# Last attention unit and first output strip of a two-layer decoder step: other order on four engines

## The reference

```
proj = u @ w_in;  q, gate = proj[..., :2048], proj[..., 2048:]
log_keep = where(mask, log_sigmoid(-z), 0);  suffix = sum of log_keep over later keys
attn = where(mask, exp(log_sigmoid(z) + suffix), 0);  o = attn @ v
out = (o * silu(gate)) @ w_out;   x = x + rms_norm(out, g_post)
```

## Time and profile before

| | |
|---|---|
| median of 3 runs | 1904.2 us (1903.65 to 1906.14) |
| the profiled execution's own time | 1900.16 us |
| its span | 1898.4 us |
| mean granted TensorE clock | 0.957 |
| TensorE matmuls busy | 1750.4 us (92%) |
| VectorE / ScalarE / GpSimd busy | 1107.7 / 805.4 / 248.3 us |

### The profile page before, as it was taken

One profiled execution on the slowest core, in us unless ns is written; L12 is line 12 of the kernel. 1 busy time (PEld: TensorE's weight loads), 2 busy tenths in 40 slices (PEclk: granted clock), 3 DMA queues, 4 the chain that ended last, 5 costly groups with the idle time before them and its releaser, 6 DMA issues.

```text
span 1898.4 us, 35455 instructions
## 1 busy us (share of the span) xinstructions
PE 1750.4 (92%) x13991; PEld 1681.0 (89%) x13991; DVE 1107.7 (58%) x1869; ACT 805.4 (42%) x1196; POOL 248.3 (13%) x181
## 2 busy tenths in 40 slices
PE   6999999999997999984899999999988999799994
PEld 5999999999997999973788999989887888699993
DVE  4676556666666222249577677776875656622226
ACT  4444444343445222223255555655555555522212
POOL 1000000000000001013332222222221111011110
PEclk9999999999998999995899999999999999899995
DMA  8332333323221333335221221212215777423325
GB/s 246 97 91 76 88 88 88 88 79 98 88 77 34 94 86 89 91 95 168 71 79 56 79 68 57 78 57 79 67 46 148 217 233 217 121 78 88 88 79 165
DMA packets 279214, 191.57 MB, mean 101 GB/s; under 512 B 7900, under 2 KB 250716, under 8 KB 279004
## 3 DMA queue, kind: packets, MB, share of 16 engines
q1 hardware_dynamic: 276872, 183.16, 32.9%
q0 software_dynamic: 2176, 6.69, 1.0%
q10 hardware_dynamic: 68, 0.41, 0.1%
HBM read 174.26 MB, written 15.97 MB: 100 GB/s over the span
## 4 chain that ended last, share of the span: by engine, by line
PE 76%; DVE 13%; ACT 5%; issue 4%; DMA 1%; SPq 0%; POOL 0%; ACTq 0%; DVEq 0%; POOLq 0%
PE PS L641 22%; PE PS L643 21%; PE PS L642 21%; PE Z L887 2%; DVE WS L1427 1%; PE Z L641 1%; PE Z L643 1%; PE Z L642 1%; DVE Y L1673 1%; PE Z L897 1%; DMA xin<-in_x_prompt_dram 1%; DVE T L1713 1%; PE Z L921 1%; ACT U L1238 1%; DVE T L1712 1%
## 5 line engine op out<-in xcount | busy, mean ns | idle before, releaser
L641 PE MATMUL PS<-U,WS 128*128 128x272 f32 x3680 | 1083.3, 294 | 61.0 <-DVE U L1680 34.1
L643 PE MATMUL PS<-U,WS 128*128 128x272 f32 x3680 | 1074.0, 292 | 0.0
L642 PE MATMUL PS<-U,WS 128*128 128x272 f32 x3680 | 1069.8, 291 | 0.0
L641 PEld LDWEIGHTS PS<-U,WS 128*128 128x128 f32 x3680 | 703.4, 191 | 71.8 <-issue 41.7
L642 PEld LDWEIGHTS PS<-U,WS 128*128 128x128 f32 x3680 | 703.8, 191 | 0.7
L643 PEld LDWEIGHTS PS<-U,WS 128*128 128x128 f32 x3680 | 703.0, 191 | 0.0
L1427 DVE TENSOR_TENSOR WS<-raw,WS 128x1024 fp32r<-128x1024 f32 (+1 forms) x234 | 290.3, 1241 | 430.0 <-ACT WS L1043 427.2
L1043 ACT ACTIVATE WS<-raw 128x1024 fp32r<-128x1024 f32 (+1 forms) x236 | 242.1, 1026 | 527.4 <-PE PS L643 520.6
L568 POOL TENSOR_TENSOR raw<-raw,GN 128x1024 f32<-128x1024 f32 x80 | 156.9, 1962 | 546.1 <-DMA raw<-in_b_w_in_dram 468.4
L580 POOL TENSOR_TENSOR T<-T 128x544 f32<-128x544 f32 x45 | 63.6, 1414 | 376.9 <-ACT T L1175 376.9
L577 POOL COPY T<-T 128x544 f32<-128x544 f32 x3 | 2.4, 794 | 636.4 <-ACT T L1175 578.5
(11 more groups left out here) (257 smaller groups left out, 2018.0 us busy)
## 6 DMA issues: line engine op xcount, KB each, us to landing
raw<-in_a_w_in_dram SPq DMA_DIRECT2D x80, 512.0 KB, 3.8
raw<-in_b_w_in_dram SPq DMA_DIRECT2D x64, 512.0 KB, 4.0
raw<-in_a_w_out_dram SPq DMA_DIRECT2D x32, 512.0 KB, 3.9
KPG<-in_cache_k_dram SPq DMA_DIRECT2D x64, 256.0 KB, 3.1
VPG<-in_cache_v_dram SPq DMA_DIRECT2D x64, 256.0 KB, 3.0
raw<-in_b_w_out_dram SPq DMA_DIRECT2D x32, 512.0 KB, 3.9
T<-scratch_x SPq DMA_DIRECT2D x32, 272.0 KB, 2.9
scratch_x<-T POOLq DMA_DIRECT2D x16, 272.0 KB, 3.2
```

The lines of the kernel that those rows point to most:

```text
L641: pe.matmul(psum, w_hi, x_hi, start=first, stop=False)
L642: pe.matmul(psum, w_hi, x_lo, start=False, stop=False)
L643: return pe.matmul(psum, w_lo, x_hi, start=False, stop=last)
```

## The change

The first output strip is done by token halves: both units' products with the first 272 columns, then both with the last 272. The first halves do not wait for the samples. `values(15)` and the turning of the second sums stand inside them, ahead of a tile of each. `values(15)` reads its pages from `KPG[0]` with a semaphore of its own. ScalarE and VectorE split tiles 0 to 7 and 0 to 3 of phase E's input earlier; the order of the last strip, the second unit's weights and the last silu changes; and the sigmoid's table is loaded ahead of the last sigmoid, with no reload of the exp and log tables behind it.

```
 SyncE
             def load_values(j):
+                if j == NHALF - 1:
+                    sp.wait_ge(kp_t, 4 * j)
+                    load_pages(j, KPG[0], a["cache_v"], last_values_in)
+                    return
...
 TensorE
             def values(j):
                 pe.wait_ge(d_wt_out, event(j) + 1)
-                pe.wait_ge(values_in, 64 * (j + 1))
+                if j == NHALF - 1:
+                    pe.wait_ge(last_values_in, 64)
+                else:
+                    pe.wait_ge(values_in, 64 * (j + 1))
                 for i in range(4):
-                    ins = weigh(event(j), i, VPG[:, i, :], False, j % 8 == 7)
+                    ins = weigh(event(j), i, (KPG[0] if j == NHALF - 1 else VPG)[:, i, :], False, j % 8 == 7)
...
-            for j in range(D_UNITS - PAGES_AT - 2, NHALF):
-                weights_turn(j)
-                values(j)
-            for h in range(2):
+            def sums_turn(h):
                 pe.wait_ge(d_sums, h + 1)
+                if h == 0:
+                    pe.wait_ge(kp_odd, 2 * NHALF)
+                else:
+                    pe.wait_ge(d_zout, NHALF + 1)
                 for i in range(4):
                     ins = pe.transpose((KT, SC)[h][:, i * P:(i + 1) * P], OE[h][:, i * P:(i + 1) * P], IDN[:])
                 ins.then_inc(d_turned, 1)
+            def first_half(u, h, at_tile=None):
+                pe.wait_ge(w_low, E0 + u + 1)
+                if u == 0:
+                    if h == 0:
+                        pe.wait_ge(strip_out, SE0 - 1)
+                    else:
+                        pe.wait_ge(y2_new, 1)
+                cols = slice(h * HALF, (h + 1) * HALF)
+                for c in range(UT):
+                    kt = u * UT + c
+                    if at_tile is not None:
+                        at_tile(c)
+                    pe.wait_ge(y2_low, kt + 1)
+                    ins = three_pass(PS[:, 0, h, 0:HALF], WS[:, u, 0, c, :], WS[:, u, 1, c, :], U[:, x_hi(kt), cols],
+                                     U[:, x_lo(kt), cols], kt == 0, kt == KD - 1)
+                if h == 1:
+                    ins.then_inc(unit_done, 1)
+            weights_turn(NHALF - 1)
+            sums_turn(0)
+            first_half(0, 0, lambda c: values(NHALF - 1) if c == 5 else None)
+            first_half(1, 0, lambda c: sums_turn(1) if c == 4 else None)
+            for u in range(2):
+                first_half(u, 1)
...
-                for s in range(4):
+                for s in range(2 if first else 0, 4):
...
 ScalarE
                 nc.scalar.activation(T[:, 8, 0:TOK], src, ACT.Sigmoid).then_inc(sgb_ready, 1)
-                act.preload_act_table_set("natural_log_exp_and_others")
+                if n < NH - 1:
+                    act.preload_act_table_set("natural_log_exp_and_others")
...
                     sums_copy(0)
+                if n == D_UNITS - 1:
+                    for o in range(4):
+                        y2_split(o)
                 if 1 <= j <= NHALF:
                     weight_exp(j - 1)
                 if j == 9:
                     weight_copy(9, NS)
+                if n == D_UNITS - 1:
+                    for o in range(4, UT):
+                        y2_split(o)
+                    act.preload_act_table_set("sigmoid_and_others")
...
             gate_sigmoid(D_UNITS // 2 - 1, NKV - 1, GRP - 1)
-            for o in range(UT):
+            high(E0 + 1, 1, (E0 + 1) // 2)
+            for o in range(UT, KD):
                 y2_split(o)
-            sums_copy(1)
-            for o in range(UT, KD - 1):
-                y2_split(o)
+                if o == 10:
+                    sums_copy(1)
             act.wait_ge(d_out, 1)
             nc.scalar.activation(U[:, 0:KD, SEQ:TOK], Y[:, 0:KD, SEQ:TOK], ACT.Copy).then_inc(y2_new_high, 1)
-            y2_split(KD - 1)
-            high(E0 + 1, 1, (E0 + 1) // 2)
...
 VectorE
                     silu(*STRIPS[n // 2 - 1][1:])
+                if n == D_UNITS - 1:
+                    for o in range(4):
+                        y2_rest(o)
...
             strip(D_UNITS // 2 - 1)
+            for o in range(4, UT):
+                y2_rest(o)
+            low(E0 + 1, 1)
             silu(NKV - 1, GRP - 1)
-            for o in range(KD - 1):
+            for o in range(UT, KD):
                 y2_rest(o)
...
                             ALU.subtract).then_inc(y2_new, 1)
-            y2_rest(KD - 1)
-            low(E0 + 1, 1)
```

More of the change, by code:

```diff
@@ L235, in build @@
         values_in = sem("values_in")
+        last_values_in = sem("last_values_in")
         kp_t = sem("kp_t")
@@ L1004, in _ @@
                 ins.then_inc(d_turned, 1)
+            def first_half(u, h, at_tile=None):
[21 more added lines that the diff above has]
+                first_half(u, 1)
             def pair_e(i, first):
-                for s in range(4):
+                for s in range(2 if first else 0, 4):
                     if s % 2 == 0:
                         pe.wait_ge(strip_out, i * 2 + (SE0 + s // 2 - 1))
[L1011 to L1014, removed]
                     unit(i * 4 + (E0 + s), s % 2, s // 2, range(s % 2 * UT, (s % 2 + 1) * UT), x_hi, x_lo,
-                         s % 2 == 0, s % 2 == 1, wait_tile if first and s < 2 else None)
+                         s % 2 == 0, s % 2 == 1)
             pair_e(0, True)
```

## The result

The changed kernel took 1893.01 us (median of 8 runs, 1887.94 to 1897.5), the kernel before 1902.27 in its 8 runs (1898.95 to 1906.14): ratio 0.9946, 95% interval [0.9934, 0.9958], so 8 to 12.6 us faster. The profiled execution took 1887.94 us and was the fastest of the eight; its span is 1886.2 us, the mean granted clock 0.962.

What follows compares the result with a forecast made beforehand. TensorE's matmuls fill 92% of the span; at the seam between phases D and E VectorE holds it. First halves 6.05 + VectorE's chain 0.9 + clock 0 = 6.9 us off 1904.2 gives 1897.3 us, range 1894.4 to 1899.8.

Steps and rivals of the forecast that it cites:

- VectorE's chain: VectorE's work from silu 38 to the samples sets when the second halves start: 1654.3, 0.9 us earlier than before.
- ScalarE ahead of the chain: ScalarE's splits, sigmoid and high part stay ahead of VectorE; idle time hides the 1.28 us table load.
- TensorE's first halves: 48 of phase E's first 96 matmuls move ahead of the samples and fit before 1654.3, gaining 6.05 us.
- The pages and the weights of E0+2: Pages for values(15) land before TensorE wants them; unit E0+2's weights stay hidden with 0.6 us to spare; no cost.
- The clock at 1654.3: TensorE's clock entering the second halves, the open term: half clock as before, so 0 gained; full clock adds 1.71 us.
- the case I feared: A clock fall in the second halves: about 3 us of half clock on the path, leaving 6.9 us gained.
- The number to subtract from: The kernel before's median over the runs, 1904.2 us, from which the 6.9 us gain was taken.
- the first rival: Full clock through all second halves, 1.71 us on top: 8.6 us gained, 1895.6 us; chance 0.32.
- late pages: Before the samples, values at half clock and a page late: part of a rival losing 1 to 4 us, chance 0.15.
- late weights: Slot 0's weights arriving after the strip's end: part of the same rival losing 1 to 4 us, chance 0.15.
- mere shift of the pause: TensorE's second halves wait as long as both halves did before; time stays within 0.2%; chance 0.03.
- The slower case: values(15)'s pages land so late that the samples are delayed, up to 4.7 us slower, 1908.9 us; chance 0.02.

Runs made afterwards that it cites:

- silu_first: Changed kernel with VectorE doing strip 39, silu 39 and the low part of E0+1 before all sixteen rests; ratio 0.9966 to the kernel before.
- samples_early: Changed kernel with the samples' products behind VectorE's rest 11, their rest behind rest 13, and the second sums' turning ahead of tile 9; 1891.63 us, ratio 0.9941.
- after_again: Changed kernel run again without any edit, to see whether its trace repeats; 1892.58 us against 1903.7 for the kernel before, ratio 0.9948.
- late_table: Changed kernel with the sigmoid's table load not ahead of time but at the last sigmoid; ratio 0.9956 to the kernel before.
- whole_filled: Changed kernel's queues, but TensorE does the first strip whole, with 36 extra matmuls in its wait for the samples; last weight turning to strip 0's end 28.20 us.
- shared_pages: Changed kernel with the last event's value pages in the one value buffer, as in the kernel before; ratio 0.9939 to the kernel before.
- after_filled: Changed kernel with 16 extra matmuls in TensorE's pause ahead of tile 8; last weight turning to strip 0's end 23.78 us.
- before_filled: Kernel before with 32 extra matmuls in TensorE's last wait ahead of phase E; last weight turning to strip 0's end 29.32 us.
- before_again: Kernel before, run again without any edit for a second trace; last weight turning to strip 0's end 31.98 us.
- pool_rests: As samples_early, with GpSimd doing the rests of tiles 0 to 7 and VectorE strip, silu, low part, then rests 8 to 15; ratio 0.9968.
- whole_strip: Changed kernel, but TensorE does the last values, both sum turnings, then the first strip whole; other queues stay changed; 1899.07 us, ratio 0.9992.

## Why the prediction was right and wrong

**VectorE's chain: right, a little short.** I forecast 0.9 us; the start moved from 16.94 to 15.57 and 15.75, 1.2 to 1.4 us. Some 0.3 us of the rest are overlap of neighbouring instructions that I had counted in full. That the chain decides is shown by silu_first (+2.45 us) and samples_early (-0.58, or -0.41 against after_again).

**ScalarE ahead of the chain: right**, but the cover that I named for the table load was not needed. In late_table the load stood at the sigmoid and was hidden all the same, under the wait for the strip.

**TensorE's first halves, 6.05 us: right.** They fit in every trace; whole_filled against the changed kernel gives 6.2.

**The pages and the weights of E0+2: right**, both at nothing. No wait for either shows in the changed kernel's traces, and the second buffer is not what hides the pages (shared_pages).

**The clock at 1654.3: the step that failed.** I took "one stretch of half clock on the path as the likelier case", and so a difference of nothing against before. Instead three of three traces of the changed kernel have the full clock in the second halves: 6.28 us against the first unit's 7.76 and 8.98 in the two traces of before. Twice the fall came early, under VectorE's pace, once not at all; after_filled shows that the case I feared exists, and its 1.5 us. I read two single pauses as if their length decided. The second error is in the same term: I priced the slow start at 1.71 from one trace. By the first unit at full clock (6.32 in before_filled) it cost 1.44 there, and 2.66 in before_again; and for the same reason the second halves at full clock end 6.28 us after their start, not 6.05. The term is worth 1.5 to 2.7 us, not 0. Why the clock falls behind some of these pauses and not behind others stays open.

**The sum with what was measured:** 6.05 (first halves) + 1.2 to 1.4 (chain) + 1.5 to 2.7 (clock), or 30.75 or 31.98 less 22.0, gives 8.7 to 10.0 us. Both ratios, about 10 us with intervals of 8 to 12.6 and 7.4 to 12.6, hold that. What more there may be, the traces do not place. Ahead of the seam the last turning of weights came at 1635.89, 1640.86 and 1641.46 in the changed kernel and at 1638.20 and 1641.36 in the one before, with no order in it; behind the seam the three spans of the changed kernel have 228.2 to 229.2 us left, the two of before 228.9 and 229.5.

**The number to subtract from.** 1904.2 was the median of three runs; over the eight runs beside the changed kernel it was 1902.27, and in the larger groups of runs later 1901.5 to 1903.7. Of the 4.3 us between 1897.3 and 1893.01, 1.9 are this base and 2.4 the gain (9.3 instead of 6.9). The range lacked the first part and ended at 1894.4, while the first rival's 8.6 us taken off 1902.27 give 1893.7.

**The other rivals.** No late pages, no late weights, no mere shift of the pause. The slower case had no support in any trace.

## What to carry to other kernels

Where TensorE waits for a small late operand that only some columns need, do the columns that do not need it first; the matmuls that move ahead of the wait are gained in full, and the work may also keep the clock up at the end of the wait, which was worth another 1.5 to 2.7 us here and came in all traces with halves but after_filled's. Price a slow start from several traces, and give the base of a forecast its own spread. Before work is handed from VectorE to GpSimd, look at what VectorE does at that moment: six of its rows took 0.6 to 1.1 us longer beside GpSimd here.

## What the runs showed of the hardware that was not expected

- The table load of the sigmoid in late_table ran as soon as ScalarE was free and did not wait for the sigmoid's data: it began 0.02 us after the instruction ahead of it, and the sigmoid 0.75 us after its end. Whether the chip or the order of the program's queue does this, no run shows.
- Pauses of TensorE of 1.9 to 2.1 us sometimes cost clock and sometimes not, with the same instructions: two of three traces of the changed kernel have a fall behind the pause of 2.10 us, the third has none behind 2.10 or 1.91, silu_first has none behind 1.91, and after_filled has one behind 1.91. Shorter ones do not rule it out: shared_pages has a fall behind 1.73 us, and pool_rests has two, beside pauses of 1.12 and 1.13.
- Leaving half clock after a long wait cost 1.4, 2.2 and 2.7 us for the same 48 matmuls (7.76, 8.48 and 8.98 us in before, whole_strip and before_again, against 6.32 and 6.34 in before_filled and whole_filled).
- The same kernel reaches the seam at times that are 5.6 us apart (1635.89 and 1641.46), and over all fourteen traces the time at half clock up to 1630 us goes from 95 to 116 us. The later arrivals tend to have more of it (116 us in the latest, shared_pages at 1643.83), which was not tested by an experiment.
